# Four arriving slots and four high-half buffers in place of five and three, in a two-block transformer kernel

## The chip, the cores and the metric

The kernel runs on one core of one Trainium2 chip. The metric is the device time of one execution in microseconds (us), the median of several runs. TensorE multiplies, VectorE and ScalarE do elementwise work, GpSimd issues the small transfers, and SyncE issues the stream of weights.

## What is computed

Two blocks in float32 over 256 tokens of width 2048, one after the other. Most of the time goes into products with weights that are read once: each is loaded, used for the 256 tokens, and dropped.

```
def first_block(x, ...):
    a = rms_norm(x, attn_norm); proj = a @ w_in
    h = x + concatenate([mla_attention(...), swa_sink_attention(...)]) @ w_out
    h = h + square(relu(rms_norm(h, mlp_norm) @ w_up)) @ w_down        # 2048 -> 8192 -> 2048
    return rms_norm(h, final_norm)

def second_block(x, c, ...):
    sh1, sc1, g1, sh2, sc2, g2 = split(silu(c) @ w_ada + b_ada, 6)     # w_ada 2048 x 12288
    z = (x * (1 + sc1) + sh1) @ w_in + b_in
    y_a = spatial_gating(...) @ w_branch_a;  y_b = hyena(...) @ w_branch_b
    mix = (gate_a * y_a + gate_b * y_b) @ w_o + b_o
    x = layer_norm(ALPHA * x + g1 * mix, ln1_g, ln1_b)
    f = square(relu((x * (1 + sc2) + sh2) @ w_m1 + b_m1)) @ w_m2 + b_m2
    return layer_norm(ALPHA * x + g2 * f, ln2_g, ln2_b)
```

## The kernel before

**Tiles.** All large weights come as one stream of 402 weight tiles of 128 x 2048 floats (1 MB each), numbered w = 0 to 401: the first block's projections up to 41, its MLP 42 to 169, the second block's projections 170 to 273, its MLP 274 to 401. An MLP has four quarters of 32 tiles, 16 "up" tiles and then 16 "token" (down) tiles. Between them stand 96 extra items, rows of w_ada, 1 MB each too. VectorE alone uses them: one multiplication with a sum each (`condition`, line 1926), written back over the slot. `stream_order` puts extra item number a behind weight tile step + 2 for each step in `COND_STEPS`; in long stretches that is every second step, so the order of arrival is: even tile, extra, odd tile, even tile, extra, odd tile.

**Slots and buffers.** An item is loaded into one of `RING` = 5 slots of 8 KB per partition (`stage`), the item at place n of the order into slot n % RING. TensorE runs its float32 products as a high and a low part of the weights. ScalarE copies the tile rounded into a high buffer (`w_hi`, `HIGH` = 3 buffers, line 1127); VectorE then writes tile minus high part over the slot itself (`w_lo` lies on `stage`, line 1604). So a slot is free when TensorE has finished its tile (`tile_done`), or for an extra when VectorE has (`ada_mac`); a high buffer is free when TensorE has finished the tile that used it.

**Who waits for what.** SyncE issues the loads in the order of arrival (lines 472 to 482): the load at place n waits until the item at place n - RING is done. ScalarE's and VectorE's queues are written out by hand: in step w both first split tile w + 2, then do the rest of step w. ScalarE's copy waits for the tile to have landed and for `tile_done` to reach `freed(w)`. VectorE's queue is: low part of w + 2, the extra behind w + 2 if there is one, then in the last step of a unit the work on TensorE's result. After an odd "up" tile that work is `take_up`: ScalarE takes the cross terms (L1385), VectorE adds (L1940) and squares (L1941), ScalarE makes the high half of the result (L1388), VectorE the low half (L1943). TensorE waits for `lo_ready` of a tile before it starts it.

**Seams.** At the end of the first block (tiles 168, 169, then 170, 171) and ahead of the second MLP (272, 273, then 274, 275) two tiles are multiplied together, by halves of the tokens (`last_tiles`, then `first_tiles`): the first half of both, the second half of both. Tile 168 counts as done when its second half is, after 169's first half. Meanwhile `into_stage` normalizes: VectorE adds the last result, ScalarE squares, VectorE and ScalarE make the root, both scale, TensorE turns (L775), both scale and shift, and the halves go into `xs`. In both queues this stands behind the split of tile w + 2 of the last step; in the first seam that is tile 171. For the first tile behind each seam (170 and 274, `FIRST`) a fourth high buffer is borrowed from a place that other data hold at other times (`w_first`); that is why `slot_of` and `freed` have their corrections, and why ScalarE waits for `spectrum_stored` and `rows_used`.

**Start.** The first five loads are written out among the loads of the input; the fifth stands last of them and waits for nothing.

Of the kernel before, what the change touches and what calls it, by code (L numbers as in the profile page):

```python
# [22 lines left out]
F32R = mybir.dt.float32r  # L23
# [7 lines left out]
P = 128  # L31
# [22 lines left out]


TILE = 2048
RING = 5
HIGH = 3
T_IN, T_KR, T_QB, T_KVB, T_WOUT = 0, 18, 19, 22, 26
T_MLP1 = 42  # L60
T_Z = 170
# [3 lines left out]
FIRST = (T_Z, T_MLP2)  # L65
# [48 lines left out]

def slot_of(w):

    return (w - (w > T_Z) - (w > T_MLP2)) % HIGH


def freed(w):  # L120

    for first in FIRST:
        if first < w <= first + HIGH:
            return w - HIGH
    return w - HIGH + 1


# [98 lines left out]
def _program(nc, dram, out, ctx):  # L226
# [11 lines left out]
    def at(name, shape, dt, off):  # L238
        return nc.alloc_sbuf_tensor_at(name, shape, dt, offset=A0 + off)

    K = 1024
    stage = at("stage", [P, RING, TILE], F32, 0)
    w_lo = at("w_lo", [P, RING, TILE], F32R, 0)
    w_hi = at("w_hi", [P, HIGH, TILE], F32R, 40 * K)
    w_first = at("w_first", [P, TILE], F32R, 144 * K + 32 * K)
    xs = at("xs", [P, DC, 2 * S], F32R, 64 * K)
    out_t = at("out_t", [P, DC, S], F32, 64 * K)
    resid = at("resid", [P, NB, D], F32, 96 * K)
# [168 lines left out]

    def high(w):

        return w_first[:] if w in FIRST else w_hi[:, slot_of(w), :]  # L420

    PARTS = ((0, 0), (1, 0), (0, 1), (1, 1), (2, None), (3, None))

# [34 lines left out]
    @blk.sync  # L458
    def _(sp):
        ws = dram["wstream"]  # L460

        def load(n):
            m = columns_of(ORDER[n][1]) if ORDER[n][0] == "w" else TILE
            sp.dma_start(stage[:, n % RING, 0:m], ws[n][:, 0:m]).then_inc(loaded[n % RING], 16)

        load(0)
        sp.dma_start(cols[:], dram["cols"]).then_inc(sem("cols_loaded"), 16)
        for g in range(4):
            sp.dma_start(xraw[:, 4 * g:4 * g + 4, S:2 * S], dram["xT"][:, 4 * g:4 * g + 4]).then_inc(
                sem(f"x_loaded_{g}"), 16)  # L470
            if g % 2:
                load(1 + g // 2)
        load(3)
        for t in range(NB):
            sp.dma_start(resid[:, t, :], dram["x"][:, t, :]).then_inc(sem("tokens_loaded"), 16)
        load(4)
        for n in range(RING, len(ORDER)):
            kind, k = ORDER[n - RING]
            if kind == "w":
                sp.wait_ge(tile_done, k + 1)  # L480
            else:
                sp.wait_ge(ada_mac, k + 1)
            load(n)
        for n in range(4):
            sp.wait_ge(sem("out_vec"), n + 1)
            sp.wait_ge(sem("out_act"), n + 1)
            sp.dma_start(out[:, 4 * n:4 * n + 4], out_t[:, 4 * n:4 * n + 4]).then_inc(sem("out_stored"), 16)
        sp.wait_ge(sem("out_stored"), 16 * 4)
# [3 lines left out]
    def _(pool):  # L492
# [77 lines left out]
        pool.wait_ge(evac_done, U_MLP2)  # L570
        pool.dma_start(lg_row[:], dram["lg_row"]).then_inc(sem("rows_loaded"), 16)
        pool.wait_ge(sem("rows_loaded"), 48)
        pool.wait_ge(tile_done, T_MLP2 + 1)
        pool.dma_start(lb_row[:], dram["lb_row"]).then_inc(sem("rows_loaded"), 16)
        pool.wait_ge(sem("gate_taken"), 2)
        pool.dma_start(gates[1], gate_t[:]).then_inc(sem("gate_stored"), 16)
# [538 lines left out]
    def _(act):  # L1115
        def split(w):

            n = place(w)
            act.wait_ge(loaded[n % RING], 16 * (n // RING + 1))
            if w == FIRST[0]:  # L1120
                act.wait_ge(sem("spectrum_stored"), 64)
            elif w == FIRST[1]:
                act.wait_ge(sem("rows_used"), 1)
            elif w >= HIGH:
                act.wait_ge(tile_done, freed(w))
            m = columns_of(w)
            act.activation(high(w)[:, 0:m], stage[:, n % RING, 0:m], ACT.Copy).then_inc(hi_ready, 1)  # L1127
# [460 lines left out]
    def _(dve):  # L1588
# [707 lines left out]
        for w in range(T_WO, T_MLP2):  # L2296
# [11 lines left out]
            if k0 == 4:  # L2308
# [5 lines left out]
                for t in range(NB):  # L2314
                    ins = stt(resid[:, t, b], resid[:, t, b], ALPHA, fn_row[:, b], ALU.mult, ALU.mult)
                link(ins)
                if n == 3:
                    dve.nop().then_inc(sem("rows_used"), 1)
            if k0 == 8:
                for t in range(NB):  # L2320
                    ins = tt(resid[:, t, b], resid[:, t, b], bo_row[:, b], ALU.add)
# [235 lines left out]
```

## Time and profile before

| | us |
|---|---|
| median of 3 runs | 2406.86 |
| range of the runs | 2405.13 to 2407.28 |
| profiled execution | 2405.96 |
| its span, first to last instruction | 2404.1 |
| TensorE busy | 2365.9 (98%) |
| VectorE busy | 1722.9 (72%) |
| ScalarE busy | 1063.1 (44%) |
| read from memory | 547 MB, 232 GB/s over the span |

Busy time is the time in which an engine has an instruction in work. TensorE's matmuls are pipelined, so their single durations overlap. A wait is put down to what ended it. The span is 1.9 us shorter than the execution's own time. In the rows, PE is TensorE, DVE VectorE, ACT ScalarE, SP SyncE.

### The profile page before, as it was taken

Reading aid. Unit: us, or ns where it says so; the run is one execution under the profiler, and the core shown is the slowest. Engines: PE = TensorE matmul, PEld = TensorE weight load, DVE = VectorE, ACT = ScalarE, POOL = GpSimd, SP = SyncE. Lnnn points to the kernel's source line nnn. Section 1 sums busy time; section 2 is a strip of 40 time slices with the busy share of each in tenths; the row PEclk is TensorE's granted clock in tenths of the full one; section 3 lists DMA queues with packets and bytes.
Section 4 is the critical chain, followed back from the end, with each engine's and each line's share of the span. In section 5 each row is a group of like instructions: output and inputs, shape, how many; then the busy total and the mean of one; then the engine's idle time right before and its main releaser. Section 6 shows DMA issues by size and latency. Waiting matters only on the chain.

```text
span 2404.1 us, 30196 instructions
## 1 busy us (share of the span) xinstructions
PE 2365.9 (98%) x12960; PEld 2022.8 (84%) x12960; DVE 1722.9 (72%) x1600; ACT 1063.1 (44%) x1031; POOL 29.8 (1%) x61
## 2 busy tenths in 40 slices
PE   7999999999999999999999999999999999999998
PEld 6888888888788888878888888987888888888887
DVE  7877577878777767676787666898764566764665
ACT  5564544444334334464654444444543433443443
POOL 0000000000000000000000000000000000000000
PEclk9999999999999999999999999999999999999999
DMA  7334477777677777766655457776555567765552
GB/s 277 134 127 157 175 264 269 287 265 262 262 292 287 281 294 278 297 246 227 250 191 181 177 188 285 298 296 243 188 189 195 185 226 281 289 259 204 191 189 110
DMA packets 79813, 558.68 MB, mean 232 GB/s; under 512 B 9034, under 2 KB 11285, under 8 KB 13248
## 3 DMA queue, kind: packets, MB, share of 16 engines
q1 hardware_dynamic: 74832, 528.25, 59.1%
q0 software_dynamic: 4848, 28.50, 3.2%
q8 instruction: 102, 1.67, 0.3%
q14 instruction: 31, 0.25, 0.0%
HBM read 547.26 MB, written 9.45 MB: 232 GB/s over the span
## 4 chain that ended last, share of the span: by engine, by line
PE 94%; DVE 3%; ACT 1%; DMA 1%; issue 0%; SPq 0%; ACTq 0%; DVEq 0%
PE ps L626 33%; PE ps L629 15%; PE ps L712 12%; PE ps L714 12%; PE ps L713 12%; PE ps L624 1%; PE ps L594 1%; PE ps L595 1%; PE ps L596 1%; DMA stage<-wstream 1%; DVE w_lo L1604 1%; PE ps L1052 1%; PE ps L1042 1%; PE ps L977 1%; PE ps L775 0%
## 5 line engine op out<-in xcount | busy, mean ns | idle before, releaser
L1604 DVE TENSOR_TENSOR w_lo<-stage,w_hi 128x2048 fp32r<-128x2048 f32 x400 | 915.0, 2288 | 445.6 <-ACT w_hi L1127 441.4
L1127 ACT ACTIVATE w_hi<-stage 128x2048 fp32r<-128x2048 f32 x400 | 764.2, 1912 | 787.9 <-DMA stage<-wstream 474.9
L626 PE MATMUL ps<-xs,w_hi 128*128 128x512 f32 x3136 | 973.9, 396 | 0.0
L629 PEld LDWEIGHTS ps<-xs,w_lo 128*128 128x128 f32 x2936 | 552.0, 188 | 129.1
L629 PE MATMUL ps<-xs,w_lo 128*128 128x256 f32 x2936 | 578.2, 278 | 0.0
L626 PEld LDWEIGHTS ps<-xs,w_hi 128*128 128x128 f32 x3136 | 485.5, 189 | 11.4 <-issue 3.1
L712 PE MATMUL ps<-w_hi,hs 128*128 128x512 f32 x992 | 387.8, 391 | 0.0
L714 PE MATMUL ps<-w_lo,hs 128*128 128x512 f32 x992 | 386.2, 389 | 0.0
L713 PE MATMUL ps<-w_hi,hs 128*128 128x512 f32 x992 | 386.2, 389 | 0.0
L1926 DVE SCALAR_TENSOR_TENSOR stage<-stage,cond 128x2048 f32<-128x2048 f32 x96 | 219.3, 2284 | 2.1 <-DMA stage<-wstream 2.1
L712 PEld LDWEIGHTS ps<-w_hi,hs 128*128 128x128 f32 x992 | 186.3, 188 | 40.7 <-issue 1.8
L713 PEld LDWEIGHTS ps<-w_hi,hs 128*128 128x128 f32 x992 | 186.3, 188 | 39.2 <-issue 0.7
L714 PEld LDWEIGHTS ps<-w_lo,hs 128*128 128x128 f32 x992 | 186.3, 188 | 38.7
L1388 ACT ACTIVATE hs<-tev 128x512 fp32r<-128x512 f32 x64 | 40.5, 632 | 171.8 <-DVE tev L1941 171.8
L626 PE MATMUL ps<-xin,w_hi 128*128 128x512 f32 x288 | 93.9, 408 | 14.4 <-DVE xin L1650 12.9
L1385 ACT ACTIVATE tev<-ps 128x512 f32<-128x512 f32 x64 | 37.5, 587 | 94.1 <-PE ps L626 94.1
L1943 DVE TENSOR_TENSOR hs<-tev,hs 128x512 fp32r<-128x512 f32 x64 | 44.3, 693 | 44.7 <-ACT hs L1388 44.7
L2210 DVE TENSOR_TENSOR tev<-ps,tev 128x512 f32<-128x512 f32 x36 | 24.8, 689 | 68.7 <-ACT tev L1504 50.4
L629 PEld LDWEIGHTS ps<-xin,w_lo 128*128 128x128 f32 x270 | 52.0, 192 | 12.4
L626 PEld LDWEIGHTS ps<-xin,w_hi 128*128 128x128 f32 x288 | 45.1, 194 | 15.0 <-issue 14.8
L629 PE MATMUL ps<-xin,w_lo 128*128 128x256 f32 x270 | 54.2, 283 | 0.0
L712 PE MATMUL ps<-w_hi,xin 128*128 128x512 f32 x128 | 51.2, 400 | 0.0
(435 smaller groups left out, 2177.6 us busy)
## 6 DMA issues: line engine op xcount, KB each, us to landing
stage<-wstream SPq DMA_DIRECT2D x497, 1024.0 KB, 4.9
spectra<-k_made POOLq DMA_DIRECT2D x4, 1024.0 KB, 8.0
k_spec<-spectra POOLq DMA_DIRECT2D x4, 1024.0 KB, 6.5
xraw<-xT SPq DMA_DIRECT2D x4, 512.0 KB, 11.5
resid<-x SPq DMA_DIRECT2D x2, 1024.0 KB, 15.0
w<-w POOLq DMA_DIRECT2D x16, 128.0 KB, 5.8
parked<-resid POOLq DMA_DIRECT2D x1, 2048.0 KB, 9.7
resid<-parked POOLq DMA_DIRECT2D x1, 2048.0 KB, 7.8
```

The source lines that it names most:

```text
L626: mm = pe.matmul(out[c], hi[c], rhs[:, k, :], start=(first and j == 0), stop=end)
L629: mm = pe.matmul(out[c][:, S:2 * S], lo[c], rhs[:, k, 0:S], start=False, stop=False)
L712: pe.matmul(o2, x_hi, hi, start=(first and j == 0), stop=False)
L713: pe.matmul(o2, x_lo, hi, start=False, stop=False)
L714: mm = pe.matmul(o2, x_hi, lo, start=False, stop=(last and j == 3))
L1127: act.activation(high(w)[:, 0:m], stage[:, n % RING, 0:m], ACT.Copy).then_inc(hi_ready, 1)
L1385: act.activation(tev[:, u % 2], ps[:, b:b + 2, S:2 * S], ACT.Copy).then_inc(cross_ready, 1)
L1388: act.activation(hs[:, 2 * j:2 * j + 2, 0:S], tev[:, u % 2], ACT.Copy).then_inc(act_hi, 1)
L1604: tt(w_lo[:, slot, 0:m], stage[:, slot, 0:m], f(high(w)[:, 0:m]), ALU.subtract).then_inc(lo_ready, 1)
L1926: stt(src, src, 1.0, cond[:], ALU.mult, ALU.mult, accum_out=mod[:, a:a + 1]).then_inc(ada_mac, 1)
L1943: tt(hs[:, 2 * j:2 * j + 2, S:2 * S], t, f(hs[:, 2 * j:2 * j + 2, 0:S]), ALU.subtract).then_inc(evac_done, 1)
L2210: took(tt(t, acc(u), t, ALU.add), u)
```

## The change

`RING` becomes 4 and `HIGH` 4. The slots take 32 KB in place of 40, and the high buffers lie behind them, from 32 KB to 64 KB; the total is the same. Every tile uses high buffer w % 4, and the copy of tile w waits for tile w - 4 in every case. The borrowed buffer goes, and with it the two waits of ScalarE for it, the signal `rows_used` and GpSimd's wait for the tile ahead of the load of `lb_row`. The fifth load is no longer written out: it is the first of the loop and waits for tile 0.

```diff
-RING = 5
-HIGH = 3
+RING = 4
+HIGH = 4
 def slot_of(w):
-    return (w - (w > T_Z) - (w > T_MLP2)) % HIGH
+    return w % HIGH
 def freed(w):
-    for first in FIRST:
-        if first < w <= first + HIGH:
-            return w - HIGH
     return w - HIGH + 1
-    w_hi = at("w_hi", [P, HIGH, TILE], F32R, 40 * K)
-    w_first = at("w_first", [P, TILE], F32R, 144 * K + 32 * K)
+    w_hi = at("w_hi", [P, HIGH, TILE], F32R, 32 * K)
     def high(w):
-        return w_first[:] if w in FIRST else w_hi[:, slot_of(w), :]
+        return w_hi[:, slot_of(w), :]
@@ SyncE
-        load(4)
         for n in range(RING, len(ORDER)):
@@ GpSimd
-        pool.wait_ge(tile_done, T_MLP2 + 1)
         pool.dma_start(lb_row[:], dram["lb_row"]).then_inc(sem("rows_loaded"), 16)
@@ ScalarE, split(w)
-            if w == FIRST[0]:
-                act.wait_ge(sem("spectrum_stored"), 64)
-            elif w == FIRST[1]:
-                act.wait_ge(sem("rows_used"), 1)
-            elif w >= HIGH:
+            if w >= HIGH:
                 act.wait_ge(tile_done, freed(w))
@@ VectorE
-                if n == 3:
-                    dve.nop().then_inc(sem("rows_used"), 1)
```

## Rows read from the trace of the kernel before

**Rows 1.** The page: the chain that ended last, share of the span by engine.
```profile
PE 94%; DVE 3%; ACT 1%; DMA 1%; issue 0%; SPq 0%; ACTq 0%; DVEq 0%
```

**Rows 2.** Waits of TensorE, whole span: line, releaser, us in total, times, longest.
```profile
PE ps L626 <- DVE xin L1650: 12.9, 1, 12.9
...
PE ps L820 <- DVE prob_a L1694: 2.6, 2, 1.3
PE ps L626 <- DVE in_cross L1784: 1.4, 1, 1.4
...
PE ps L647 <- DVE w_lo L1604: 1.0, 1, 1.0
```

**Rows 3.** Waits of ScalarE's high copy, whole span, the same columns.
```profile
ACT w_hi L1127 <- DMA stage<-wstream: 474.9, 138, 9.2
...
ACT w_hi L1127 <- PE ps L714: 212.9, 69, 5.3
```

**Rows 4.** Order of time, SyncE: start us, us, instruction; ends of tiles 122 and 124.
```profile
784.55 0.80 SPq L464 DMA_DIRECT2D stage<-wstream  x2
...
795.43 0.80 SPq L464 DMA_DIRECT2D stage<-wstream  x2
```

**Rows 5.** Order of time, ScalarE, the high copies of tiles 125 and 126.
```profile
789.30 1.92 ACT L1127 ACTIVATE w_hi<-stage 128x2048 fp32r<-128x2048 f32 x1 [2.86 <-DMA stage<-wstream]
791.85 1.92 ACT L1127 ACTIVATE w_hi<-stage 128x2048 fp32r<-128x2048 f32 x1 [0.62 <-DMA stage<-wstream]
```

**Rows 6.** Order of time, VectorE, low parts: tile 126; then tiles 113 and 114.
```profile
793.80 2.29 DVE L1604 TENSOR_TENSOR w_lo<-stage,w_hi 128x2048 fp32r<-128x2048 f32 x1 [0.26 <-ACT w_hi L1127]
...
724.45 2.29 DVE L1604 TENSOR_TENSOR w_lo<-stage,w_hi 128x2048 fp32r<-128x2048 f32 x1 [0.39 <-ACT w_hi L1127]
...
730.57 2.29 DVE L1604 TENSOR_TENSOR w_lo<-stage,w_hi 128x2048 fp32r<-128x2048 f32 x1 [1.11 <-ACT w_hi L1127]
```

**Rows 7.** The slots, 695 to 1026 us: extras (ns least/median/most, first and last start), landings.
```profile
L1926 DVE SCALAR_TENSOR_TENSOR stage<-stage,cond x30: 2281/2284/2286, 696.2 to 1015.9; 128x2048 f32<-128x2048 f32 x30
...
DMA to landing us min/median/max: 4.6/4.9/8.5
```

**Rows 8.** Order of time, SyncE, ends of tiles 106 and 166.
```profile
695.35 1.34 SPq L464 DMA_DIRECT2D stage<-wstream  x2
...
1026.20 0.80 SPq L464 DMA_DIRECT2D stage<-wstream  x2
```

**Rows 9.** Order of time, SyncE, ends of tiles 324 and 352.
```profile
1965.94 0.81 SPq L464 DMA_DIRECT2D stage<-wstream  x2
...
2120.39 0.80 SPq L464 DMA_DIRECT2D stage<-wstream  x2
```

**Rows 10.** The chain that ended last in order of time, first seam, tile 171.
```profile
1031.64 4.75 DMA stage<-wstream
...
1038.37 2.29 DVE w_lo L1604
```

**Rows 11.** Order of time, first seam: SyncE (end of tile 168), TensorE.
```profile
1041.15 0.80 SPq L464 DMA_DIRECT2D stage<-wstream  x2
...
1035.36 0.50 PE L647 MATMUL ps<-w_hi,hs 128*128 128x512 f32 x1 [1.04 <-DVE w_lo L1604]
...
1044.22 0.65 PE L775 MATMUL ps<-ident,resid 128*128 128x128 f32 x4 [1.06 <-DVE resid L2062]
```

**Rows 12.** Stretch in the second seam: stretch, length, busy by engine, PEclk, DMA share, GB/s.
```profile
1684.00:1688.00 4.00, 4.00 (x22) 4.00 (x23) 3.24 (x4) 3.52 (x4) 0.00 (x0) 0.57 0.01 4
```

**Rows 13.** Order of time, second seam: SyncE (end of tile 271), ScalarE's root.
```profile
1660.94 0.33 SPq L464 DMA_DIRECT2D stage<-wstream  x1
...
1669.18 0.20 ACT L1155 ACTIVATE root__73<-var 128x1 f32<-128x1 f32 x1 [2.32 <-DVEq L1621]
```

**Rows 14.** Start: low part of tile 4; the work behind tile 3 in the chain.
```profile
34.25 2.29 DVE L1604 TENSOR_TENSOR w_lo<-stage,w_hi 128x2048 fp32r<-128x2048 f32 x1 [0.27 <-ACT w_hi L1127]
...
41.40 0.46 PE ps L856 x4
```

## The prediction

> **What bounds the kernel now.** I read the chain that ended last first: TensorE holds 94% of it [rows 1]. Then the waits: TensorE waited 12.9 us once at the start, and otherwise for single microseconds [rows 2]; in some 400 tiles it waited once for a low part, 1.0 us. So the kernel runs at TensorE's own pace, and work taken off another engine brings nothing unless it ends one of those waits. The waits of ScalarE's high-half copy say what that engine sits on: 474.9 us for the arriving tile (138 times), 212.9 us for a TensorE tile to end [rows 3]. The second is the wait that a fourth high buffer loosens; the first is the one that four slots in place of five can lengthen. Neither holds TensorE today, so the question is how much room lies between "low part ready" and "tile begins", and what the change takes of it.
>
> **Where the room is smallest.** It is where an extra tile (the 96 "a" items) arrives with every second weight tile. In such a stretch SyncE issues two loads when an even tile ends, one when the odd one ends. Take the token stretch at 784.55 us [rows 4]: tile 122 ends, SyncE issues tile 125 and right behind it tile 126. The first has landed by 789.30, 4.75 us later, the second by 791.85, 7.3 us later [rows 5]: the second of two waits for the first one's bytes, 2.5 us. The copy takes 1.92, and the low part that follows 791.85 starts at 793.80 and takes 2.29 [rows 5, 6]. So a second-of-two tile has its low part 11.55 us after the release, 11.6 with the signal to TensorE; a first-of-two 9.1. Tile 125 begins two tiles after the release, 10.88 us in token tiles (784.55 to 795.43, [rows 4]); for up tiles the stretch below leaves 11.17.
>
> **Part 1, the ring of four.** With five slots the item at place n waits for place n-5, with four for n-4. In the order "even tile, extra, odd tile, even tile, extra" this moves both: the extra, formerly released one tile earlier by the odd tile before, is now released by the end of the even tile, together with the odd tile, and is issued ahead of it (the odd tile's own slot is one that an extra leaves, free long before). The even tile is released by the next tile's end, alone. So the odd tile changes from first to second of two: its low part comes at 11.6 instead of 9.1 us after the release, while TensorE wants it at 10.88 (token) or 11.17 (up). It is late by 0.7 or 0.4 us. A late start does not add up fully: the release of the next odd tile follows the end of the tile in between, so the loop is release, 11.6 us, two tiles, release, over four tiles. Token: (11.6 + 10.88)/2 = 11.24 per pair for 10.88, a loss of 0.36.
> In up tiles one more link is tied to it. The even tile's low part follows the odd one's by 6.12 us (724.45 to 730.57, [rows 6]): the fold and the square on VectorE, the copy on ScalarE, then ScalarE's high copy and VectorE's low part, in program order. That is more than a tile of 5.58. Then the loop is 11.6 + 6.12 + 5.58 over two pairs, 11.65 per pair for 11.17, a loss of 0.49 (between 0.22, were the link absent, and 0.97, were nothing shared).
> How many pairs: between 695.35 and 1026.20 us there are 30 extras [rows 7, 8], 330.9 us. Two of the MLP's quarters lie in it, 16 up and 16 token tiles each, so 15 pairs of either kind; 15 x 10.88 for the token ones leaves 11.17 for an up pair, 5.58 a tile, with no other TensorE work between. From 1965.94 to 2120.39 [rows 9] lie 14 gaps of 11.03 on average, so the same spacing: 15 more, 8 up and 7 token. In the first half of the first MLP the filter work widens most gaps; going by SyncE's double issues 7 up and 7 token pairs stay tight; before the second seam 6 token pairs. Up 30 x 0.49 = 14.7; token 35 x 0.36 = 12.6; the remaining 31 (gaps of 11.2 to 17 us) I put at 3.5 together, between 0 and 8. **Sum 30.8 us.**
> VectorE's extra multiplication gets its data 4.8 us after the release; the engine is at the even tile's low part until about 6 us after it, so this wait is hidden; the multiplication ends at 8.4, ahead of the high copy at 9.25. Cover gone, it costs up to its 2.28 us per pair.
> Stretches without extras: a tile released three tiles ahead (16.3 us) lands in 4.8 and needs 4.2 for its two parts: nothing. On the price of a load the rows say 4.75 us for one of 1 MB and 2.5 more for the second. The Trainium skill ("DMA: Bandwidth & Descriptors", the table of fixed and variable time) has about 2.0 us fixed plus bytes over 436 GB/s, 4.4 us and 2.4 more, and so a second-of-two low part at 11.1 by estimate; token pairs would then lose 0.11 and up pairs 0.24, and the sum above would be 14.6, not 30.8. The measured 7.3 decides.
>
> **Part 2, the first seam.** Here one load changes its releaser for the worse. Tiles 168 and 169 are multiplied together, and tile 168 counts as done only in the second half. Before, tile 171 is released by tile 167's end at 1031.64, and the chain of waits shows that this very load opens the seam: 4.75 us, the copy, the low part at 1038.37, then VectorE's add [rows 10]. VectorE and ScalarE have that split ahead of the whole seam in their queues: add, square, root, scaling, turn and the two next tiles wait behind it. With four slots, tile 171 (place 230) waits for place 226, tile 168. Tile 168 ended at 1041.15 [rows 11]. It will end later: tile 169's low part, for which TensorE waited 1.04 us until 1035.36 [rows 11], is a second-of-two now, 1026.20 + 11.6 = 1037.8, 2.4 later. So the release comes at 1043.6 instead of 1031.64, **12.0 us**, and since the chain hangs on it without slack, the seam moves by as much. TensorE, which waited 1.06 us ahead of its first turn [rows 11], then stands there some 10.6 (1.06 and 12.0, less the 2.4 already spent). In the second seam, where TensorE also waits for such a chain, the granted clock fell: 0.57 of 2.4 GHz on average in 1684 to 1688 us [rows 12], so 1.2 GHz for most of it and 1.7 us of work lost. I add **1.7 us** for the same here (0 to 3). The Trainium skill ("TensorE: Matmul & The Clock Gate", The HAM clock gate) has the array fall back to 1.2 GHz after idling; the second seam agrees.
> Bounds of the seam: 9.6 if tile 169 were not later, 15 with the clock at its upper bound.
>
> **Part 3, the second seam.** No extras near it: tile 275 is released by tile 271's end, 1660.94 [rows 13], instead of a tile earlier; landed 1665.7, copied 1667.7, root table 1669.0. ScalarE's root follows a 2.32 us wait at 1669.18 [rows 13], which hides it, by 0.2 us. Nothing, at most 0.5. The borrowed buffer's two waits and GpSimd's wait for tile 274 go; TensorE waits for none of them.
>
> **Part 4, the fourth high buffer.** In the tight pairs the copy waits for the load or, in up tiles, for its place in ScalarE's queue, so the buffer is inert. Elsewhere the copy moves a tile earlier. What it can end on TensorE: 2.6 us for probabilities and 1.4 for the projection [rows 2], where ScalarE's queue could run ahead; I take 0 (bounds 0 and -4.0), since the copy sat beside VectorE's maximum, not on it. The fifth load at the start is issued when tile 0 ends instead of ahead of it; tile 4's low part was made from 34.25 on and tile 3 ran until 41.40 [rows 14], so it may land 4.8 us later at no cost: 0.
>
> **Sum:** 30.8 + 12.0 + 1.7 = 44.5 us on the profiled execution's 2405.96 us (span 2404.1 and 1.9 around it): 2450.5. That execution lies 0.9 under the median of 2406.86, within the three runs; I predict 2450.
>
> **Rivals.** (a) *The pairs hold, only the seam pays.* If the odd tile lands before the even deadline (low part by 10.9), only part 2 and some of the other pairs pay: 2406 + 13.7 and 3.5, 2423. Against it: the 7.3 us of [rows 5]. The Trainium skill's price for a load, above, points halfway there. (b) *The lateness is not shared between pairs.* If something re-times each release to the late start (a scattered landing, up to 8.5 us [rows 7], or the multiplication slipping between the two low parts), each pair pays in full: 35 x 0.72 + 30 x 0.97 + 3.5 = 58, with the seam 2406 + 58 + 13.7 = 2478. (c) *Faster:* the fourth buffer lets ScalarE's queue run ahead in attention and ends the 4.0 us of TensorE's waits named in part 4, and the ring costs nothing because the loads are still in time: 2406 - 4 = 2402. It decides from the point where a second-of-two low part is ready within 10.9 us of its release and tile 171 arrives before 1031 + 5; the rows say 11.6 and 1048. (d) *It does nothing:* all is hidden, 2406.
>
> **How the numbers follow.** Forecast 0.66 (own range 2438 to 2462: links 0.22 or 0.6 for 0.49, other pairs 0 to 8, seam 9.6 to 15), (a) 0.14, (b) 0.13, (c) 0.03, (d) 0.04. The range reaches to both neighbours in part: 2430 to 2472. A measurement of this kernel can tell 0.2%, 5 us, from no change: faster 0.03, same 0.04, slower 0.93.
>
> **What would show it.** Right: TensorE gains waits for low parts, 0.3 to 0.8 us each in up and token stretches with extras and none in those without; the stretch of 30 extras grows from 330.9 to about 344 us; SyncE's double issue is then extra and odd tile; ahead of the first seam's turn TensorE idles about 10 us, with the clock at its lower level after it; ScalarE's 212.9 us of waits for TensorE shrink and nothing follows. Wrong: the stretch keeps 331 us (then (a)), or grows beyond 355 ((b)), or the first seam's shift is a few us, which would say that its chain did not hang on that load.

## The result and the profile after

The changed kernel takes **2516.5 us** (median of 4 runs, 2511.8 to 2521.3) against 2406.2 for the kernel before (2405.1 to 2407.3): the ratio is 1.046, with an interval of 1.0447 to 1.0472. The prediction had 2450 and a range up to 2472. Slower was right; 44 us were forecast and 110 came. The profiled execution has a span of 2514.6 us for 2404.1.

The chain that ended last, on the page of the changed kernel, answers to [rows 1]:

```profile
PE 71%; DMA 13%; DVE 9%; ACT 5%; issue 2%; SPq 0%; ACTq 0%; DVEq 0%
PE ps L620 24%; DMA stage<-wstream 12%; PE ps L623 11%; PE ps L706 9%; PE ps L708 9%; PE ps L707 9%; DVE w_lo L1594 5%; ACT w_hi L1117 4%; PE ps L588 1%; PE ps L589 1%; PE ps L590 1%; PE ps L618 1%; PE ps L1046 1%; DVE stage L1916 1%; PE ps L971 1%
```

TensorE held 94% of it. Now a fifth (12, 4 and 5%) is a load, its high copy and its low part, in that order, again and again: at these places the arriving tile sets the pace. The waits of TensorE (line, releaser, us in total, times, longest) answer to [rows 2]. The line numbers have moved by 6 for TensorE (L626 is L620, L712 is L706), by 4 for SyncE and by 10 for VectorE and ScalarE.

```profile
PE ps L706 <- DVE w_lo L1594: 25.3, 27, 2.6
PE ps L620 <- DVE w_lo L1594: 18.8, 32, 2.8
PE ps L620 <- DVE xin L1640: 12.9, 1, 12.9
PE ps L769 <- DVE resid L2052: 10.7, 1, 10.7
PE ps L660 <- DVE xs L2070: 7.7, 4, 2.7
PE ps L588 <- DVE tev L2279: 7.0, 3, 2.9
PE ps L620 <- DVE tev L2258: 4.6, 2, 2.3
...
PE ps L706 <- issue: 2.9, 1, 2.9
PE ps L588 <- DVE tev L2258: 2.9, 2, 2.3
```

Low parts were waited for once in the kernel before, 1.0 us; now 59 times on the two main lines, 44.1 us. The 10.7 us is the first seam. The three lines with L2258 and L2279, 14.5 us, were no part of the prediction: there TensorE waits for a *result* of VectorE in the branch tiles (242 to 271). The waits of ScalarE and VectorE answer to [rows 3]:

```profile
ACT w_hi L1117 <- DMA stage<-wstream: 886.0, 249, 11.5
```
```profile
DVE w_lo L1594 <- ACT w_hi L1117: 470.4, 265, 10.1
DVE stage L1916 <- DMA stage<-wstream: 70.2, 46, 6.0
```

ScalarE waited 474.9 us for arriving tiles, now 886.0, and its waits for a TensorE tile (212.9 us in [rows 3], and 99.7 on two smaller lines of that list) are gone. L1916 is VectorE's multiplication of the extra; it stood idle for 2.1 us in the whole kernel before, by its page, and waits 70.2 us for extras now.

**Where the 110 us are.** The ends of the tiles, from TensorE's signals up to the last tile, set against those of the kernel before, with the prediction's terms by stretch:

| stretch | predicted | measured |
|---|---|---|
| start, attention (tiles 0 to 46) | 0 | -0.4 |
| first MLP (47 to 167) | 18.7, and most of 3.5 | 47.5 |
| first seam (168 to 170) | 13.7 | 13.3 |
| tiles 171 to 241 | part of 3.5 | 3.8 |
| branches and output (242 to 271) | 2.2 | 36.2 |
| second seam (272 to 275) | 0 | -1.1 |
| last MLP | 6.4 | 11.6 |
| whole | 44.5 | 110.9 |

### The profile page after: what moved, and what is told of

The parts are those of the page before. It is cut to its first block, busy times and chain, and to the rows that moved or that the text cites. A ratio compares the mean times of both kernels' runs of the same rounds, so it can differ in the third digit from the quotient of the medians.

```text
span 2514.6 us, 30193 instructions
## 1 busy us (share of the span) xinstructions
PE 2402.3 (96%) x12960; PEld 2031.1 (81%) x12960; DVE 1724.6 (69%) x1600; ACT 1061.9 (42%) x1031; POOL 29.9 (1%) x61
## 4 chain that ended last, share of the span: by engine, by line
PE 71%; DMA 13%; DVE 9%; ACT 5%; issue 2%; SPq 0%; ACTq 0%; DVEq 0%
PE ps L620 24%; DMA stage<-wstream 12%; PE ps L623 11%; PE ps L706 9%; PE ps L708 9%; PE ps L707 9%; DVE w_lo L1594 5%; ACT w_hi L1117 4%; PE ps L588 1%; PE ps L589 1%; PE ps L590 1%; PE ps L618 1%; PE ps L1046 1%; DVE stage L1916 1%; PE ps L971 1%
## 5 line engine op out<-in xcount | busy, mean ns | idle before, releaser
L1117 ACT ACTIVATE w_hi<-stage 128x2048 fp32r<-128x2048 f32 x402 | 767.6, 1911 | 887.2 <-DMA stage<-wstream 886.0
L620 PE MATMUL ps<-xs,w_hi 128*128 128x512 f32 x3136 | 981.4, 398 | 18.8 <-DVE w_lo L1594 18.8
L620 PEld LDWEIGHTS ps<-xs,w_hi 128*128 128x128 f32 x3136 | 484.5, 189 | 40.2 <-DVE w_lo L1594 30.3
L706 PE MATMUL ps<-w_hi,hs 128*128 128x512 f32 x992 | 391.9, 395 | 21.0 <-DVE w_lo L1594 21.0
L1916 DVE SCALAR_TENSOR_TENSOR stage<-stage,cond 128x2048 f32<-128x2048 f32 x96 | 219.7, 2288 | 70.4 <-DMA stage<-wstream 70.2
L706 PEld LDWEIGHTS ps<-w_hi,hs 128*128 128x128 f32 x992 | 186.6, 188 | 73.1 <-DVE w_lo L1594 33.2
L620 PE MATMUL ps<-xin,w_hi 128*128 128x512 f32 x288 | 93.7, 407 | 14.4 <-DVE xin L1640 12.9
L623 PEld LDWEIGHTS ps<-xin,w_lo 128*128 128x128 f32 x270 | 51.9, 192 | 12.4
L620 PEld LDWEIGHTS ps<-xin,w_hi 128*128 128x128 f32 x288 | 45.1, 194 | 14.8 <-issue 14.8
L706 PE MATMUL ps<-w_hi,mixs 128*128 128x512 f32 x112 | 46.1, 412 | 7.2 <-DVE w_lo L1594 4.3
```

Of the source, the lines that this page charges most:

```text
L620: mm = pe.matmul(out[c], hi[c], rhs[:, k, :], start=(first and j == 0), stop=end)
L623: mm = pe.matmul(out[c][:, S:2 * S], lo[c], rhs[:, k, 0:S], start=False, stop=False)
L706: pe.matmul(o2, x_hi, hi, start=(first and j == 0), stop=False)
L1916: stt(src, src, 1.0, cond[:], ALU.mult, ALU.mult, accum_out=mod[:, a:a + 1]).then_inc(ada_mac, 1)
```

## The experiments

The losses by stretch in them all, worked out in the same way from each profiled execution (us over the kernel before):

| run | time, median | first MLP | first seam | 242 to 271 | last MLP | whole |
|---|---|---|---|---|---|---|
| the change | 2516.5 | 47.5 | 13.3 | 36.2 | 11.6 | 110.9 |
| e1 ring of four alone | 2520.5 | 52.2 | 11.6 | 33.2 | 11.7 | 113.7 |
| e2 tiny extras | 2427.9 | 4.4 | 10.7 | 5.8 | 0.0 | 22.0 |
| e5 half extras | 2495.5 | 35.1 | 15.5 | 29.9 | 8.9 | 90.9 |
| e4 no extra at 168 | 2505.3 | 51.9 | 0.9 | 32.1 | 11.3 | 99.7 |
| e3 results ahead of extras | 2500.7 | 48.2 | 13.2 | 18.1 | 11.3 | 93.3 |
| e6 both | 2488.5 | 52.7 | 0.0 | 15.0 | 11.9 | 85.1 |
| e7 extras behind odd tiles | 2506.5 | 44.1 | 4.7 | 29.5 | 11.8 | 94.9 |
| e9 odd tile issued first | 2475.7 | 14.2 | 11.6 | 37.8 | 2.0 | 67.9 |
| e10 all three | 2433.5 | 16.5 | 0.1 | 4.7 | 0.3 | 23.9 |
| e8 before, no extra at 168 | 2403.7 | 0.4 | -2.6 | -1.0 | 0.0 | -4.3 |
| e11 before, with both repairs | 2403.8 | 0.4 | -1.1 | 0.5 | 0.0 | -0.3 |

From the same edit to another profile a stretch moves by 1 to 4 us, so smaller differences in this table say nothing.

**e1: the ring without the buffer.** The kernel before with four slots and its three high buffers.

```diff
-RING = 5
+RING = 4
-        load(4)
```

> The kernel before with four slots in place of five and nothing else: three high buffers and the borrowed one stay. Theory 1 (the ring alone makes the loss, the fourth high buffer is inert): 2516 us, within 3 of the changed kernel. Rival (the fourth buffer gives some of it back, or its later copies cost): it differs from the changed kernel by 5 us or more; since in the stretches with an extra behind every second tile the copy waits for its load and not for a buffer, I hold to 2516.

2520.5 us, ratio 1.0475 (1.0459 to 1.0490); the change has 1.0459 (1.0447 to 1.0472). The 4 us between them lie between the two theories, and the intervals overlap. So the slot that was given up makes the loss, and the fourth high buffer is worth 4 us at most here. It did what it was meant to: with three buffers ScalarE's high copy still waits 242.6 us for TensorE tiles, with four not at all, and TensorE gains nothing that can be told from it. Whether it would bring something where all loads are in time was not tried by itself.

**e2: tiny extras.** The changed kernel with the extras' bytes all but gone.

```diff
-            m = columns_of(ORDER[n][1]) if ORDER[n][0] == "w" else TILE
+            m = columns_of(ORDER[n][1]) if ORDER[n][0] == "w" else 64
-                stt(src, src, 1.0, cond[:], ...)
+                stt(src, cond[:], 1.0, cond[:], ...)
```

> The changed kernel, but each of the 96 extras loads 64 of its 2048 columns, and VectorE multiplies the conditioning vector with itself in their place (same length of instruction, same waits, same order of release); so what the extras compute is left out. It parts bytes from order. Theory 1 (an odd tile is late because it lands 2.5 us after the extra that is issued ahead of it): both MLPs' stretches with extras lose nothing (they lose 47.6 and 11.5 us now), the first seam keeps about 11 of its 13, the branch stretch (tiles 242 to 271, 36 us now) keeps little, since a small extra lands about 2.3 us after its release in place of 4.8: 2425 us (2418 to 2435). Rival (the later release itself costs, whatever the bytes): 2480 or more.

2427.9 us (ratio 1.0088, 1.0071 to 1.0106), as Theory 1 had it. With the order of loads and slots unchanged, the loss of the MLPs falls from 47.5 and 11.6 to 4.4 and 0.0 us: it comes from the bytes of the extras. They work in two ways that this run does not part: the odd tile behind them lands later, and VectorE gets the extra itself later. Across the first MLP the second of the two loads lands 5.32 us after the release (median), for 7.28 in the changed kernel. What stays is above all the seam. These waits of TensorE are of this run:

```profile
PE ps L769 <- DVE resid L2052: 10.5, 1, 10.5
...
PE ps L620 <- DVE w_lo L1594: 2.8, 5, 1.1
```

**e3: the results ahead of the extra, tiles 242 to 273.** In the branch stretch the changed kernel shows this on VectorE, then on TensorE, in order of time (start, us, engine, line):

```profile
1638.98 2.29 DVE L1916 SCALAR_TENSOR_TENSOR stage<-stage,cond 128x2048 f32<-128x2048 f32 x1 [2.37 <-DMA stage<-wstream]
...
1641.99 0.69 DVE L2279 TENSOR_TENSOR tev<-ps,gate_b 128x512 f32<-128x512 f32 x1
```
```profile
1642.83 0.36 PE L588 MATMUL ps<-y_b,w_hi 128*128 128x256 f32 x1 [2.91 <-DVE tev L2279]
```

VectorE stands 2.37 us for an extra that is still under way, multiplies it for 2.29, and only then takes the result, which holds a bank of TensorE's output memory (PSUM); TensorE, which needs the bank, has been idle for 2.91. In this run the multiplication stands behind the results:

```diff
         for w in range(T_BA, T_BB):
             split(w + 2)
-            condition(w + 2)
 ...
             tt(mixacc[:, c:c + 2, :], mixacc[:, c:c + 2, :], t, ALU.mult).then_inc(evac_done, 1)
+            condition(w + 2)
```
(and in the same way in the two loops behind it)

> The changed kernel, with VectorE's multiplication of the extra moved behind its work on TensorE's result in tiles 242 to 273, where every tile or nearly every one is a unit of its own. Theory 2 (there VectorE stands waiting for the extra, which now lands 4.8 us into the next tile, and the result behind it in its queue is taken too late for TensorE's next unit in that bank): the stretch of tiles 242 to 271 loses 6 to 10 us in place of 36, total 2487 us (2482 to 2495), no waits of TensorE for L2279 and L2258. Rival (late low parts make that stretch's loss, as in the MLPs): under 5 us gained, 2512.

2500.7 us (1.0388, 1.0367 to 1.0409). The stretch loses 18.1 us in place of 36.2, where Theory 2 had 6 to 10 and the rival more than 31: the mechanism is there and makes half of this stretch's loss. TensorE's waits for the two results fall from 14.5 to 5.1 us and do not vanish. Of the next two waits the first below is of the changed kernel from 1556 to 1761 us, the second of this run from 1557 to 1744, VectorE in both.

```profile
DVE stage L1916 <- DMA stage<-wstream: 29.2, 10, 6.0
```
```profile
DVE stage L1916 <- DMA stage<-wstream: 2.1, 2, 1.9
```

**e4: no extra at tile 168.** The last extra of the first MLP moves to a gap of the next stage.

```diff
-COND_MLP1 = (..., *range(64, 125, 2))
-COND_Z = (4, 6, 14, 18, 20, 22)
+COND_MLP1 = (..., *range(64, 123, 2))
+COND_Z = (4, 6, 10, 14, 18, 20, 22)
```

> The changed kernel, with the extra behind tile 168 moved behind tile 182, so that tile 171 is released by tile 167's end again and tile 169 comes alone. Theory 3 (the first seam hangs on the load of tile 171): tiles 168 to 170 give their 13.2 us back, less what tile 180 to 184 may lose (0 to 1), 2503 us (2500 to 2507), and the half clock in and behind the seam goes. Rival (the seam is late for another cause, such as the fourth buffer's order or slots still held by the two double tiles): under 4 us gained.

2505.3 us (1.0406, 1.0383 to 1.0428), as expected; the seam's 13.3 us fall to 0.9, and TensorE's wait of 10.7 at its first turn to

```profile
PE ps L769 <- DVE resid L2052: 2.4, 1, 2.4
```

**e5: half extras.** As e2, with 1024 columns.

```diff
-... else TILE
+... else 1024
```

> The changed kernel with extras of 1024 columns in place of 2048 (512 KB a load); the multiplication is as long as before but reads the condition in place of the slot, so the extras' sums are left out of what is computed. In the changed kernel the first MLP lost 47.6 us; with extras of 64 columns 4.2. Theory 1 (steady lateness by the loop of the prediction): the extra's bytes ahead of the odd tile fall from 2.5 us to 1.25, the odd tile's low part comes 10.35 us after its release, ahead of the deadlines of 10.88 and 11.17 in every pair: the first MLP loses what it does with tiny extras, 4 to 6 us, and the whole stands near 2435. Theory 2 (scattered landings, each late start priced by itself): landings spread over 2.5 us in the changed kernel, so a shift of 1.25 leaves part of the pairs late: the first MLP loses 10 to 20 us and the whole stands near 2450. Theory 3 (the order of the loads and not their bytes): nothing falls, 2515.

2495.5 us (1.0373, 1.0359 to 1.0387): neither 2435 nor 2450, and not 2515. What failed is the premise of the first two. The issues of this run (KB each, median us to landing):

```profile
stage<-wstream SPq DMA_DIRECT2D x401, 1024.0 KB, 4.9
stage<-wstream SPq DMA_DIRECT2D x97, 512.0 KB, 4.4
```

Half the bytes take 4.4 us and not 3.5; the odd tile behind lands 7.04 us after the release in place of 7.28 (medians in the first MLP). So 0.24 us less, and the first MLP loses 12.4 us less. With tiny extras it is 1.96 us less and 43.1 us. The loss goes with the landing of the odd tile, and is steepest where it just misses; the extra's own landing moves with it (see e2).

**e6: e3 and e4 together.**

> The changed kernel with both repairs: no extra at tile 168 (moved to tile 10 of the first stage), and in the branch's tiles the extra is multiplied behind the tile's own results. One alone gave 2505.3 and the other 2500.7, against 2516.5. If they are separate mechanisms their gains add: 11.2 and 15.8, so 2489. If the branch's pairs lose only because the seam left the loads behind, or the other way round, the gains overlap and it stands near 2500.

2488.5 us (1.0339, 1.0323 to 1.0354), for 2489. The two gains add, so these are two separate mechanisms.

**e7: extras behind odd tiles.** As e4, and in the first MLP the extras lie one tile later and are multiplied behind the tile's results.

```diff
-COND_MLP1 = (*range(2, 25, 2), 26, 28, ..., *range(64, 125, 2))
+COND_MLP1 = (*range(3, 26, 2), 27, 29, ..., *range(65, 124, 2))
 ...
             split(w + 2)
-            condition(w + 2)
 ...
                 take_up(u, False)
+                condition_late(w)
```
(and in the same way behind the other work of a step)

> The changed kernel without the extra at tile 168, and in the first MLP the extras lie behind odd tiles and are multiplied behind the tile's results. The even tile is then the second of two loads. Theory 1 (the link from the odd tile's low part through the fold, the copy and the high copy, 6.1 us, ties the two tiles of an up pair): with the even tile second, a late low part is followed by the odd tile's 6.1 us later all the same, so up pairs lose about as before, 0.6 each or more, and token pairs 0.7 to 0.9: near 2505. Theory 2 (the link matters only with the odd tile late, since the even tile's extra time lets the odd one's low part come early): up pairs fall to about 0.4 and the first MLP loses some 10 us less: near 2495. Tile 171 becomes a second of two here, so the first seam may pay up to 2.5 us in either case.

2506.5 us (1.0422, 1.0406 to 1.0438), near Theory 1's 2505: the tight stretch (tiles 106 to 167) loses 29.3 us for 27.8 in e4. Moving the second of two to the other tile of the pair does not cure the loss. As the place of the multiplication moved too, the run does not show that either edit alone is without effect.

**e8: the kernel before, no extra at tile 168.** The diff of e4, with five slots.

> The kernel before, five slots, with the extra at tile 168 moved to tile 10 of the first stage. If tile 171's load opens the first seam, as the chain of waits of the kernel before says, and is released by tile 166 in place of 167 once an extra less lies ahead of it, then the seam starts earlier by the wait of 1.06 us at the first turn and by what of the 1.04 us wait for tile 169 falls: 1 to 2.5 us less than 2407, near 2405. If the seam does not hang on that load, no change. The same edit gave 11.2 us with four slots.

2403.7 us (11 runs) for 2406.7 (15), ratio 0.9990 (0.9982 to 0.9999); the seam is 2.6 us shorter. This is the quickest version of this study, by an amount too near to no change to lean on.

**e9: the odd tile issued ahead of the extra.** The same four slots; where an extra and an odd tile come together and the odd tile's slot was an extra's, SyncE issues them in the other order.

```diff
-        for n in range(RING, len(ORDER)):
+        issue = list(range(RING, len(ORDER)))
+        for n in range(RING, len(ORDER) - 1):
+            if ORDER[n][0] != "w" and ORDER[n + 1][0] == "w" and ORDER[n + 1 - RING][0] != "w":
+                issue[n - RING], issue[n + 1 - RING] = n + 1, n
+        for n in issue:
```

> The changed kernel, same four slots and same slot for every load; only SyncE's order differs: where an extra and an odd tile were issued together at the even tile's end, the odd tile is issued ahead of the extra, when the extra that holds its slot has been multiplied, 8.4 us after the release before by the prediction's steps and so some 2.5 us ahead of the even tile's end. No load is then the second of two. If the loss in the MLPs is the lateness of the odd tile, it goes: first MLP 47.6 to about 5 us, last MLP 11.4 to about 1. The first seam keeps its price (tile 171 is still released by tile 168), 11 to 13. In the branch stretch the extra comes no earlier than in the changed kernel, so VectorE's waits for it stay and with them 18 us of the 36 or more: together 2407 + 5 + 12 + 18 to 36 = 2442 to 2460. If instead the loss is a matter of four slots as such (bytes in flight, the clock), little goes and it stays above 2490.

2475.7 us (1.0290, 1.0276 to 1.0304), 16 us above the expected range. First MLP 47.5 to 14.2, last MLP 11.6 to 2.0, with the slots and bytes unchanged: the loss of the MLPs was largely the order in one strict queue, where the odd tile's load stood behind the extra's wait and behind its bytes, though its own slot was free. The first MLP keeps 14.2 us where 5 were expected, and the branches 37.8, a little above their 18 to 36. VectorE still takes the extra ahead of the odd tile's low part and now stands 132.8 us for extras in place of 70.2; whether that is the rest of the MLP's loss is asked in e13.

**e10: all three edits.** e3, e4 and e9.

> All three edits on the changed kernel: the odd tile issued ahead of the extra, no extra at tile 168, and in the branch's tiles the extra multiplied behind the tile's results. If these three are the whole loss, four slots cost 0 to 10 us and this stands at 2407 to 2417. If the fourth high buffer is worth anything once the loads are in time, it stands below the kernel before with the same two edits (the next run), 2400 or less.

2433.5 us (1.0120, 1.0104 to 1.0135), where 2407 to 2417 was expected. The three carry 83 of the 110 us; 27 stay, 16 of them in the first MLP. **e11**, the kernel before with the edits of e3 and e4, is the control:

> The kernel before, five slots, with the two edits of the repaired versions: no extra at tile 168, and the extra multiplied behind the results in the branch's tiles. The seam edit alone gave 2403.7 against 2406.7. VectorE waited 2.1 us in all for extras there, and no result was late, so the second edit brings 0 (at most -1, at worst +2 where a later multiplication releases a slot later): 2403 to 2405. This is the control for both repairs and the mark that four slots would have to beat.

2403.8 us (0.9991, 0.9982 to 1.0000): with five slots the order of extra and result is worth nothing that can be told.

**e12: the price of a late start by itself.** The kernel before, with VectorE work put ahead of six low parts of the last MLP (`DELAY` has the columns of each piece).

```diff
+            for c in DELAY.get(w, ()):
+                link(tt(cond[:, 0:c], stage[:, slot, 0:c], f(high(w)[:, 0:c]), ALU.subtract))
             tt(w_lo[:, slot, 0:m], stage[:, slot, 0:m], f(high(w)[:, 0:m]), ALU.subtract).then_inc(lo_ready, 1)
```

> The kernel before with six low parts of the last MLP's token tiles delayed by extra VectorE work ahead of them (tiles 359, 362, 365, 368, 394, 398), in a stretch where the low part is ready 6.55 us ahead of its tile: delays of about 6.3, 6.6, 6.9, 7.3, 8.1 and 9.2 us, so that it is ready 0.2 us before TensorE wants it, and 0.05, 0.3, 0.7, 1.5 and 2.6 us late. It measures by itself what a late start costs. If TensorE loses only the lateness, the six tiles last 5.44 us and 0, 0.05, 0.3, 0.7, 1.5 and 2.6 more, and the kernel grows by some 5 us, 2412. If a stopped TensorE needs some 0.3 us to come back, as the late tiles of the changed kernel suggest, each late one lasts 0.3 more and the first a little, 7 us in all, 2414. If the clock falls after the longer waits, 1.7 us more for each.

2415.7 us (1.0041, 1.0027 to 1.0055), nearest to the second forecast, 2414; the granted clock did not fall behind any of the six. From the signals of the trace, us (late: low part ready behind the end of the tile before; a token tile takes 5.44):

| tile | 359 | 362 | 365 | 368 | 394 | 398 |
|---|---|---|---|---|---|---|
| late | -0.10 | 0.17 | 0.43 | 0.89 | 1.69 | 2.76 |
| tile longer by | 0.26 | 0.56 | 0.83 | 1.25 | 2.09 | 3.13 |
| beyond lateness | 0.26 | 0.39 | 0.40 | 0.36 | 0.40 | 0.37 |

Each stop costs 0.38 us on top of its length, whatever that is. TensorE at tile 362 shows where it lies:

```profile
2169.52 0.39 PE L715 MATMUL ps<-w_hi,hs 128*128 128x512 f32 x1
2169.75 0.39 PE L716 MATMUL ps<-w_lo,hs 128*128 128x512 f32 x1
2170.36 0.50 PE L714 MATMUL ps<-w_hi,hs 128*128 128x512 f32 x1 [0.23 <-DVE w_lo L1608]
2170.70 0.40 PE L715 MATMUL ps<-w_hi,hs 128*128 128x512 f32 x1
```

Matmuls follow one another every 0.23 us though each lasts 0.39, so in a running stream the next tile begins 0.16 us before this one "ends"; and after a stop the first spacing is 0.34 in place of 0.23. These are 0.27 of the 0.38; the other 0.11 stays open. The wait in the row, 0.23 us, shows little of the 0.56 that the tile lasts longer.

**e13 and e14: what e10 still loses.** The extra's multiplication, in the first MLP, behind the odd tile's low part (e13), then behind the results of the tile too (e14).

```diff
-            condition(w + 2)
+            if w > T_MLP1:
+                condition(w + 1)
```

> As the run with all three edits (2433.5), and in the first MLP the extra is multiplied one tile later, behind the odd tile's low part in VectorE's queue. There the low part waited for the multiplication, and that for an extra that lands up to 8 us after its issue. Theory 1 (VectorE's queue is the rest of the loss): the low part follows its high copy at once, some 4 us earlier; the next odd tile's load is issued 1.5 us later, which has room; the first MLP's loss falls from 16 us to 0 to 4, and the whole stands at 2417 to 2422. Theory 2 (the scattered landings of the loads themselves): the loss stays at 10 us or more, 2428 or above.

> As the run with all three edits (2433.5), and in the first MLP the extra is multiplied at the end of the tile's VectorE work: behind the odd tile's low part and behind the fold and the result. Theory 1 (VectorE's queue is the rest): neither the odd nor the even tile's low part waits for the extra any more; its slot comes free up to 4 us later, for a load with some 3 us to spare; the first MLP's loss falls from 16 us to 0 to 5, and the whole stands at 2417 to 2423. Theory 2 (the loads' scattered landings are the rest): the loss stays at 10 us or more, 2428 or above.

In e13 the time that Theory 1 gave did not come; Theory 2's did (2428 or above), which does not show its cause. In e14 neither explains the time. e13 gives 2434.7 us (1.0117, 1.0101 to 1.0134): no gain. What Theory 1 said of the odd tiles' low parts holds, they are early now, but VectorE shows the next link (start, us; 974.49 is the extra):

```profile
972.28 2.29 DVE L1598 TENSOR_TENSOR w_lo<-stage,w_hi 128x2048 fp32r<-128x2048 f32 x1 [0.72 <-ACT w_hi L1121]
974.49 2.28 DVE L1920 SCALAR_TENSOR_TENSOR stage<-stage,cond 128x2048 f32<-128x2048 f32 x1
...
976.70 0.69 DVE L1934 TENSOR_TENSOR tev<-ps,tev 128x512 f32<-128x512 f32 x1
```

The fold stands behind the extra, ScalarE's square behind the fold and the even tile's high copy behind that, so of the 23 tiles that lose time in this stretch 22 are even, where e10 had 7 of 16. e14 gives 2533.6 us (1.0518, 1.0503 to 1.0532), the worst of all: the slot comes free at the multiplication's end, and the next odd tile is loaded into it. That load starts at 1012.76, is copied from 1017.72, and its low part starts at

```profile
1019.67 2.29 DVE L1598 TENSOR_TENSOR w_lo<-stage,w_hi 128x2048 fp32r<-128x2048 f32 x1 [4.74 <-ACT w_hi L1121]
```

ready at 1021.97, while the tile before had ended at 1020.84. Load, two parts, fold and multiplication close a loop of some 14 us (this low part starts 14.2 us behind that of the pair before, at 1005.51) for a pair of 11.17. My "3 us to spare" counted the slot's next load as wanted a pair later than it is. None of the three places tried for the multiplication (ahead of the odd tile's low part, behind it, behind the results) is free of cost in an up pair with four slots; where the remaining 16 us of e10 come from is not settled. Nine of its 16 late or nearly late tiles landed 6.7 us or more after their issue, where the median is 4.9, so the scatter probably takes part; the rest I leave open.

## Why the prediction was right and wrong

The sign, the seams and the way in which a tile comes late were right; the sum was 66 us short. Of these 34 lie in the branch tiles, where VectorE's wait for the extra was taken as hidden; some 25 to 29 in the first MLP and 5 in the last, where the price of a stop stood at nothing and the late landings nearly so.

**The ring of four: mechanism right, size wrong.** The double issue, the landing and the low part came as worked out. Tile 139 of the changed kernel (SyncE, ScalarE, VectorE, TensorE, in order of time), against [rows 4 to 6]:

```profile
896.41 0.80 SPq L460 DMA_DIRECT2D stage<-wstream  x2
```
```profile
903.64 1.92 ACT L1117 ACTIVATE w_hi<-stage 128x2048 fp32r<-128x2048 f32 x1 [6.09 <-DMA stage<-wstream]
```
```profile
905.59 2.29 DVE L1594 TENSOR_TENSOR w_lo<-stage,w_hi 128x2048 fp32r<-128x2048 f32 x1 [2.13 <-ACT w_hi L1117]
```
```profile
907.94 0.73 PE L620 MATMUL ps<-xs,w_hi 128*128 128x512 f32 x2 [0.56 <-DVE w_lo L1594]
```

Release at 896.41, landing 7.23 later (7.3 predicted), low part ready at 907.88, 11.5 later (11.6). The link in an up pair is there as well: the low parts of tiles 147 and 148 start at 952.29 and 958.41,

```profile
952.29 2.29 DVE L1594 TENSOR_TENSOR w_lo<-stage,w_hi 128x2048 fp32r<-128x2048 f32 x1 [1.43 <-ACT w_hi L1117]
...
958.41 2.29 DVE L1594 TENSOR_TENSOR w_lo<-stage,w_hi 128x2048 fp32r<-128x2048 f32 x1 [1.11 <-ACT w_hi L1117]
```

6.12 us apart, as in [rows 6]. Yet the stretch of 30 extras [rows 8] grew from 330.9 to 354.9 us (717.10 to 1072.03) and not to 344. By tile: 24 late ones with 12.9 us of lateness together, where the prediction had 12.8 for the same stretch; and on top 9.7 us that these tiles lasted longer than their lateness, and 1.4 in six that were within 0.2 us of being late. Of the 9.7, 1.9 are tile 109 alone, which ran at the lower clock (732 to 736 us, below); the other 23 tiles have 0.34 each. **The missing term is the stop itself**, 0.38 us by e12. In the loop of a token pair it counts by half: (11.6 + 0.38 + 10.88)/2 gives 11.43, a loss of 0.55 for 0.36, and in the same way 0.68 for 0.49 in an up pair. Fifteen pairs of each make 18.4 us. The last 5.6 of the 24 I put down to loads that landed later than 7.3 us and to the clock; they were not measured apart. So the agreement of 12.9 with 12.8 is in part luck. And the link works otherwise than drawn in tiles 142 to 156: there all eight even tiles are late, by 0.1 to 0.3 us, and of the odd ones only 147, by 0.02.

**The other pairs, 3.5 us with a bound of 8: wrong.** Tiles 47 to 105 lost 22.1 us, of which the seven and seven tight pairs explain 6 at the prediction's price. I called a pair with a gap of over 11.2 us nearly free, because I took a landing of 7.3 us for all. Over the first MLP the second of two lands after 7.28 us in the median but after 7.57 in the mean, 9.81 at most; 22 of 55 odd tiles are late, some by 1 to 2.8 us. So a pair that is in time at the median landing still loses at a late one, and its loss has to be read from the tail of the landings.

**"VectorE's wait for the extra is hidden": right in the MLP's pairs, wrong where it cost most.** This is the step that failed by most, 36.2 us for 2.2. I priced the branches as token pairs. But there each tile makes a result of its own, on VectorE behind the extra (e3), so the cover that I named for the MLP is not there. I had written its price, "up to its 2.28 us per pair", and not asked in which stretches it applies. e3 shows it to be half of the 36.2 us; with the odd tile's load ahead as well (e10) 4.7 remain, while that order alone (e9) takes nothing off.

**The clock: named at one place, paid at many.** In the kernel before TensorE's granted clock is at the lower level (1.2 GHz) for 9.7 us of the span, in the changed one for 55.5, in twelve stretches (the clock's rows begin at 19 us). At half pace the difference is 23 us of work at most, an upper bound, as TensorE stood idle in part of them. In e10 it is 13.4 us: the clock's loss went with the waits. Two of the stretches, by the granted clock (columns as in [rows 12]):

```profile
732.00:736.00 4.00, 4.00 (x16) 3.35 (x15) 2.20 (x3) 2.91 (x3) 0.00 (x0) 0.57 0.71 299
...
1674.00:1681.00 7.00, 5.93 (x14) 4.75 (x15) 6.72 (x8) 4.83 (x4) 0.00 (x0) 0.51 0.31 126
```

In tiles 242 to 271 it is 23.9 us at that level, up to 11.9 lost, beside 23.9 us of waits: together about the 36.2, though waits and low clock overlap in part.

**The first seam: right, in size and in detail.** 13.3 us for 13.7. Counted from tile 167's end, tile 171's release comes 12.1 us later (12.0 predicted) and TensorE's first turn 12.2; behind it another 1.1 goes, for which 1.7 had been put down to the clock. The chain of the changed kernel in order of time, against [rows 10, 11]:

```profile
1072.03 0.33 SPq L460
...
1072.40 6.93 DMA stage<-wstream
...
1079.36 1.93 ACT w_hi L1117
...
1081.31 2.30 DVE w_lo L1594
...
1083.65 0.80 PE ps L641
```

Tile 169's low part is ready 11.58 us after its release (11.6 predicted), tile 171 is issued with tile 168's end at 1091.00, its low part starts at 1097.84, and

```profile
1103.69 1.11 PE L769 MATMUL ps<-ident,resid 128*128 128x128 f32 x4 [10.68 <-DVE resid L2052]
```

where 10.6 was predicted. The granted clock is at its lower level from 1097.2 to 1107.5 us, after TensorE had stood since 1093.0 (columns as in [rows 12]):

```profile
1097.00:1107.00 10.00, 3.25 (x11) 2.45 (x11) 5.87 (x12) 5.42 (x11) 0.62 (x2) 0.51 0.06 26
```

The Trainium skill ("TensorE: Matmul & The Clock Gate", The HAM clock gate) has TensorE's array at 1.2 GHz when it idles, and this trace agrees. e4 takes the one extra away that sets this releaser, and 0.9 us remain. **The second seam and the fourth buffer:** nothing, as predicted (-1.1; e1).

**The price of a load.** The rows' 7.3 us held: tile 139 has 7.23. The Trainium skill's table ("DMA: Bandwidth & Descriptors", Anatomy of one DMA), with which the sum would have been 14.6 us for 30.8, gives an estimate of 3.2 us for a load of 512 KB, and e5 shows 4.4. The page fits that table to loads that GpSimd issues; these are SyncE's, so the prediction used it outside what it describes.

**The rivals.** (b), lateness not shared, was the nearest (2478), by a sum that did not hold either. The stretch's growth stopped just short of its mark of 355 us. Its reason was named, scattered landings, but its price took a full 7.3 us for every pair, and it knew neither the stop nor the branches. The lateness *was* shared: tiles 125 and 129 are 0.46 and 0.57 late, tile 127 between them is not.

## What to carry to other kernels

When a ring loses a slot, write down for each load what releases it now, and for each engine's queue what stands behind the wait for it: here half of the loss was late tiles in the MLPs, and half of another third came where results queued behind a side job whose data came late. A stage that just misses its deadline pays for each miss the stop of TensorE and at times its clock: in the stretch of 30 extras 12.9 us of lateness cost 24. Issue first what is wanted first: the order of two loads was worth 41 us here without a byte or a buffer.

## What the runs showed of the hardware

- A stop of TensorE costs 0.36 to 0.40 us beyond the lateness, from 0.2 to 2.8 us of lateness (e12), 0.34 on average in the changed kernel, and a low part that is ready 0.1 us ahead of the end of the tile before still costs 0.26.
- A wait of 2.07 us (tile 169) and one of 2.80 (before 731.03) were followed by the lower clock; one of 2.82 in e12 was not: the granted clock there reads

```profile
2375.00:2379.00 4.00, 3.19 (x14) 2.64 (x15) 4.00 (x4) 0.00 (x0) 0.00 (x0) 1.00 0.00 0
```

  Nor did the clock fall behind tile 92 of the changed kernel, 2.57 us late. So the length of the wait alone does not decide; what does was not tried.
- A load of 512 KB takes 4.4 us where 1 MB takes 4.8 and 32 KB 1.7: between these sizes the time does not follow the bytes.
- The second of two loads of 1 MB, issued together, lands 7.2 us after the release at best, 7.28 in the median, 7.57 in the mean and 9.8 at most (first MLP of the changed kernel). Why the landings scatter was not tried.
